# A hybrid attention layer with its SBUF tiles placed by a rule: moving operands at multiples of 64 bytes, stationary ones 32 bytes past

## What is computed

```python
h = rmsnorm(x, norm_g)
proj = jnp.einsum('bsd,dc->bsc', h, w_in)                 # 1024 -> 6656 columns
a_qkv, z_a, b_qkv, z_b, r_a, r_b = jnp.split(proj, offs, axis=-1)
# branch A: 3 groups x 4 heads, banded attention at dilation 1, 4, 16, groups mixed by their softmax sums
y_a = einsum(attn_a * silu(z_a), w_pa)                    # 256 -> 1024
# branch B: 8 heads; at 512 positions every query sees all its past blocks: causal attention
y_b = einsum(attn_b * silu(z_b), w_pb)                    # 512 -> 1024
merged = sigmoid(r_a + b_merge[:1024]) * y_a + sigmoid(r_b + b_merge[1024:]) * y_b
return rmsnorm(x + einsum(merged, w_out), final_g)
```

## The kernel before

| tile | used as | address modulo 64 |
|---|---|---|
| `w_hi`, `w_lo` | stationary; moving in v steps | 0 |
| `gat_hi`, `gat_lo` | moving | 0 |
| `hT_hi`, `hT_lo` | moving; stationary in v steps | 32 |
| `wo_a`, `wo_b` (hi, lo) | moving | 32 |
| `mrg_hi`, `mrg_lo` | stationary | 32 |
| `KTs`, `pT` | moving | 32 |
| `QTs`, `V_split_even` (`V_split_odd`) | stationary | 32 (0) |

## Times and profile before

### The profile page before, as it was taken

One profiled execution on the slowest core, in us unless ns is written; L12 is line 12 of the kernel. 1 busy time (PEld: TensorE's weight loads), 2 busy tenths in 40 slices (PEclk: granted clock), 3 DMA queues, 4 the chain that ended last, 5 costly groups with the idle time before them and its releaser, 6 DMA issues.

```text
span 463.8 us, 6276 instructions
## 1 busy us (share of the span) xinstructions
PE 448.8 (97%) x2417; PEld 381.7 (82%) x2417; DVE 216.3 (47%) x345; ACT 190.9 (41%) x388; POOL 167.5 (36%) x106
## 2 busy tenths in 40 slices
PE   8899999999999999999799999899999999999995
PEld 7689998898889888987678888688888888888885
DVE  3981244013203255668977767904307065074433
ACT  6733553144314353567326554323323263242211
POOL 3645332423234233555425552434435336300000
PEclk9999999999999999999899999899999999999998
DMA  8822242025311232032022022213422273320331
GB/s 287 258 90 92 93 136 92 1 92 137 92 35 58 93 92 87 11 98 93 6 85 75 17 69 71 70 41 92 136 92 90 90 231 110 136 92 0 116 111 45
DMA packets 38444, 43.07 MB, mean 93 GB/s; under 512 B 3448, under 2 KB 35216, under 8 KB 38416
## 3 DMA queue, kind: packets, MB, share of 16 engines
q1 hardware_dynamic: 35968, 42.47, 28.2%
q10 hardware_dynamic: 2448, 0.21, 0.4%
HBM read 39.48 MB, written 2.15 MB: 90 GB/s over the span
## 4 chain that ended last, share of the span: by engine, by line
PE 89%; DVE 7%; ACT 2%; issue 1%; DMA 1%; DVEq 0%; ACTq 0%
PE ps L702 18%; PE ps L706 18%; PE ps L703 18%; PE ps L746 4%; PE ps L747 4%; PE ps L748 4%; PE ps L906 3%; PE ps L904 3%; PE ps L905 3%; PE ps L801 3%; PE ps L848 3%; PE ps L821 3%; PE ps L805 2%; PE ps L838 2%; ACT squares L941 1%; DVE gat_lo L1221 1%
## 5 line engine op out<-in xcount | busy, mean ns | idle before, releaser
L630 POOL TENSOR_TENSOR w_lo<-raw,w_hi 128x1024 fp32r<-128x1024 f32 (+1 forms) x59 | 139.4, 2363 | 199.4 <-ACT w_hi L921 192.9
L702 PE MATMUL ps<-hT_hi,w_hi 128*128 128x512 f32 x336 | 138.4, 412 | 6.1 <-DVE KTs L1158 2.5
L706 PE MATMUL ps<-hT_lo,w_hi 128*128 128x512 f32 x336 | 134.2, 399 | 0.0
L703 PE MATMUL ps<-hT_hi,w_lo 128*128 128x512 f32 x336 | 133.9, 399 | 0.0
L702 PEld LDWEIGHTS ps<-hT_hi,w_hi 128*128 128x128 f32 x336 | 64.1, 191 | 19.0 <-issue 2.7
L706 PEld LDWEIGHTS ps<-hT_lo,w_hi 128*128 128x128 f32 x336 | 63.7, 190 | 15.4
L703 PEld LDWEIGHTS ps<-hT_hi,w_lo 128*128 128x128 f32 x336 | 64.1, 191 | 11.7
L921 ACT CAST w_hi<-raw 128x1024 fp32r<-128x1024 f32 (+1 forms) x59 | 60.1, 1018 | 19.7 <-PE ps L706 17.0
L746 PE MATMUL ps<-w_hi,hT_hi 128*128 128x256 f32 x160 | 46.0, 288 | 0.0
L748 PE MATMUL ps<-w_lo,hT_hi 128*128 128x256 f32 x160 | 44.7, 279 | 0.0
L747 PE MATMUL ps<-w_hi,hT_lo 128*128 128x256 f32 x160 | 44.7, 279 | 0.0
(11 more groups left out here) (140 smaller groups left out, 658.1 us busy)
## 6 DMA issues: line engine op xcount, KB each, us to landing
raw<-in_w_in SPq DMA_DIRECT2D x25, 1024.0 KB, 5.0
raw<-in_w_out SPq DMA_DIRECT2D x4, 1024.0 KB, 4.8
xs<-in_x SPq DMA_DIRECT2D x4, 512.0 KB, 5.0
raw<-in_w_pb SPq DMA_DIRECT2D x4, 512.0 KB, 4.0
res<-in_x SPq DMA_DIRECT2D x4, 512.0 KB, 4.0
out<-weighted SPq DMA_DIRECT2D x8, 256.0 KB, 2.1
raw<-in_w_in SPq DMA_DIRECT2D x2, 512.0 KB, 8.3
raw<-in_w_pa SPq DMA_DIRECT2D x4, 256.0 KB, 3.0
```

The costliest lines, as they stand in the source:

```text
L630: nc.gpsimd.tensor_tensor(ring(w_lo, n, kt), src, ring(w_hi, n, kt).bitcast(F32), ALU.subtract).then_inc(lo_ready, 1)
L702: pe.matmul(out, wh, hh, start=(k == 0), stop=False)
L703: pe.matmul(out, wl, hh, start=False, stop=False)
L706: return pe.matmul(out, wh, hl, start=False, stop=(k == kts - 1))
```

## The change

The weight ring's slots become 16 floats (64 bytes) longer, and `ring` starts 8 floats (32 bytes) into the slot, except for v steps, whose slots start at 0 as before (`pair_ring` is left as it is). A new tile `line_pad` of 32 bytes, never used, stands behind `unread` and brings the small tiles to 512 bytes. A new tile `mrg_skew` of 32 bytes, never used, stands ahead of `mrg_hi`.

```diff
+SKEW = 8
...
-        w_hi = sb("w_hi", [P, NRING, KT_D * P], F32R)
-        w_lo = sb("w_lo", [P, NRING, KT_D * P], F32R)
+        w_hi = sb("w_hi", [P, NRING, SKEW + KT_D * P + SKEW], F32R)
+        w_lo = sb("w_lo", [P, NRING, SKEW + KT_D * P + SKEW], F32R)
...
         unread = sb("unread", [P, 1], F32)
+        line_pad = sb("line_pad", [P, 8], F32)
...
         wo_a_lo = sb("wo_a_lo", [P, 5, D], F32R)
+        mrg_skew = sb("mrg_skew", [P, SKEW], F32)
         mrg_hi = sb("mrg_hi", [P, ND, SEQ], F32R)
...
         def ring(t, n, kt):
-            return t[:, n % NRING, 0:kt * P].rearrange("p (k c) -> p k c", k=kt)
+            at = 0 if step_kind(n) == "v" else SKEW
+            return t[:, n % NRING, at:at + kt * P].rearrange("p (k c) -> p k c", k=kt)
```

## The result

| | before | after |
|---|---|---|
| median of 22 runs each, us | 466.71 | 468.53 |
| lowest and highest | 464.03, 468.4 | 465.39, 469.79 |
| span of the profiled execution | 463.8 | 465.4 |

The ratio after to before is 1.0044, with a 95% interval of 1.0025 to 1.0062: 2.1 us slower, between 1.2 and 2.9 (the two medians as they stand are 1.8 us apart). That is within 1%, the side that the prediction held likeliest, and the move is under its sum of +3.3 us.

The account below looks back on a forecast made before the run. The prediction took PE, busy 97% of the span, as the bound. Its terms, 0.9 + 1.1 - 0.2 + 1.6 - 0.1 = +3.3 us, took the profiled 465.67 to 469.0 us; the range was 454 to 473.

Parts of the forecast that it names:

- PE's distance is what the change can move: Whole kernel: no instruction is added, so any effect is on the time from one matmul start to the next.
- the zero that was costed: ACT's and POOL's writes into ring slots 32 bytes past the multiple: claimed to add 0.
- M0 S32: Moving tile at 0, stationary at 32 bytes modulo 64; for all 1320 large matmuls after, forecast 233.3 ns, chance 0.45.
- M32 S0: Moving tile at 32, stationary at 0 bytes modulo 64: `hT` past the ring before, 233.3 ns.
- The single sample at 414.26: Step into the output projection: last `gat` matmul while `mrg` weights load, distance 0.24 against 0.23 with ring weights.
- The agreement of 227.0 and 226.8: `gat` and `wo`, both with equal places, agree to 0.2 ns; taken as a reason that only the difference counts.
- the terms of `hT` (0), `gat` (+0.9) and `wo` (+1.1): 512-column matmuls, in us: 1008 `hT` unchanged at 233.3 ns, 144 `gat` +6.3 ns each, 168 `wo` +6.5 ns each.
- Rivals 1, 2 and 3: Large matmuls at 220.5 ns (chance 0.20); M0 always 227.0 whatever S (0.18); M0 S32 worse still, 239.8 (0.10).
- rival 4: Change does nothing: `hT` and `gat` differ by their tiles, not their places; 467.0 us, chance 0.07.
- The v term: 480 v matmuls moved to equal places at 256 columns, 116.6 to 120.0 ns: +3.4 ns each, +1.6 us.
- the -0.2: 48 `wo` matmuls of 256 columns, from 120.0 ns to the v steps' 116.6: -0.2 us.
- The two streams lie 32 bytes apart modulo 64: Rule for moving and stationary operands at 512 columns: equal places modulo 64 fast, unequal ones slow, 233.3 ns.

Follow-up runs that it names:

- h_64: Kernel before plus only a `line_pad` of 96 bytes, putting `hT` 64 bytes past the ring modulo 256, ring slots unchanged: 462.07 us against 466.05, ratio 0.9914.
- a_pad: Kernel before plus only the 32-byte `line_pad`, making all operand differences 0 modulo 256: 462.63 us against 465.88, ratio 0.9938.
- b_skew: Kernel before plus the change's ring (longer slots, 32-byte shift except v steps), without `line_pad` and `mrg_skew`: ratio 1.0008 to before.
- d_vskew: Kernel before plus `line_pad` and the change's longer slots, with only v-step weights shifted 32 bytes: ratio 0.9998 to before; 0.986 was expected.

## Why the prediction was right, and where it wasn't

- **PE's distance is what the change can move.** Right. PE's share of the chain stayed 89%, and ACT and POOL kept 1049 and 2445 ns, the zero that was costed. (Of POOL's 168.8 us of idle time in the earlier trace rows, 162.3 were for ACT, not all.)
- **The missing pair, M0 S32, is as slow as M32 S0.** Right: 233.2 to 234.3 in `hT`, `gat` and `wo`. The single sample at 414.26, 0.24 us, told the truth, but that was luck: the same passage in h_64, from `gat` at 128 to `mrg` at 192 modulo 256, has 410.92 to 411.14, 0.22 us, where long stretches at that difference have 233.5 ns. The agreement of 227.0 and 226.8 was the better reason. So the terms of `hT` (0), `gat` (+0.9) and `wo` (+1.1) came out as summed. Rivals 1, 2 and 3 wanted 220.5, 227.0 and 239.8 and are out; rival 4 went with a_pad.
- **The v term was mis-sized.** The sum put +3.4 ns on each, from the 120.0 of equal places; it became +1.9 on average, 0.9 us in place of 1.6. a_pad shows that 120.0 is right for tiles equal modulo 256. In after the two slots that a v matmul reads lie 64 bytes apart modulo 256, so at most one of them can be equal to `hT`. The pairs of steps where one was ran at 118.5 to 119.0, 118.7 in the stretch above, and those where neither was at 119.5 to 120.0. The `wo` matmuls of 256 columns gave 1.5 ns each, not 3.4: -0.07 for the -0.2. Together the terms measured make +2.8 for +3.3. The ratio makes it 2.1, the estimate from runs at like clock 2.9.
- **"The two streams lie 32 bytes apart modulo 64" was the wrong rule.** This is the step that failed, without cost to the number. The rows of before allow no finer rule than "equal or not", since they hold two differences only, 0 and 32. I took the modulus from the change's own wording; b_skew, d_vskew and h_64 refute it. After shows M0 S32 slow under either rule, since all its differences are odd multiples of 32; had the change set both operands at multiples of 64 in slots of 4160 bytes, my rule would have promised the 6.4 us of d_vskew's expectation; d_vskew has those slots, and its time did not move (0.9998).
- **Against the pages.** Moving tiles by 4 bytes costs 5.8 to 6.7 ns (226.7 to 232.5 and 233.4), by 8 bytes 4.0 one way and 6.7 the other, by 32 bytes 6.6. The Trainium skill's page "SBUF — State Buffer", section "Specifications (TRN2)", counts penalties in 16-byte cachelines; by that a shift of 16, 32 or 64 should be free, and the trace doesn't bear it out for PE's operands: 32 and 64 bytes gave 233.3 and 233.5.

## What is settled and what is open

Shown: at full clock the distance of these matmuls depends on the two operands' start addresses relative to each other, and at 512 columns only 0 modulo 256 reached 226.7 ns steadily. Argued, not shown: that it is the next weight load, running beside the stream, that gets in its way. What speaks for it is that only the relation of the two counts, and that slow-clock matmuls stand at 427 ns, exactly their columns, with no surcharge. No run took the weight load away. Not explained: why 192 is 4.6 ns better than 64, why equal places are not the quick ones at 2 x 128 columns, and what picks one of several patterns for one and the same pair of addresses.

## What to carry to other kernels

When rows of back-to-back matmuls bound a kernel, compare the start-to-start distance of the same shape with different tiles; a few ns between them can be the tiles' addresses. For moving tiles of 512 columns, make each stationary tile start at the same place modulo 256 bytes as the tile that moves past it (at 2 x 128 columns that was the slow place, 120.0 ns), and keep the stride of a ring's slots a multiple of 256: a pad of one small tile was worth 2.9 us here, while slots 64 bytes longer lost all or part of it again in three slots of four. Where a rule is fitted to two values, as mine was, a run that steps through more values comes before any rule about the modulus.

## What was not expected of the hardware

- A shift of 4 bytes between the operands moves a 512-column matmul's distance from 226.7 to 232.5 or 233.4 ns.
- After other matmuls or a clock fall, up to ten matmuls pass before 226.7 is reached, and a step can then stay on another distance (227.0 or 233.4 at difference 16; 228.9 or 233.3 at 192).
- v matmuls of 2 x 128 columns ran between 113.3 and 120.0 ns, no place slower than equal, and at 113.3 or 117.8 with the same two addresses.
- The kept traces hold 5 to 15 `hT` matmuls at 1.2 GHz, worth 1 to 3 us, as much as the whole change, and the 22 runs of after alone spread over 4.4 us.
